# Both attention stages of a hybrid layer: low halves moved to GpSimd, and second operands of VectorE moved to PSUM

## What is computed

```python
def block(args):                      # group A, stick-breaking
    i, qi = args
    q_pos = i * Q_BLOCK + jnp.arange(Q_BLOCK)
    z = jnp.einsum('bhqd,bhkd->bhqk', qi, k).astype(jnp.float32) * inv_sqrt_d
    strict = key_pos[None, :] < q_pos[:, None]
    log_keep = jnp.where(strict, jax.nn.log_sigmoid(-z), 0.0)
    after = lax.cumsum(log_keep, axis=3, reverse=True) - log_keep
    w = jnp.where(strict, jnp.exp(jax.nn.log_sigmoid(z) + after), 0.0)
    return jnp.einsum('bhqk,bhkd->bhqd', w.astype(v.dtype), v)
...
    p = jax.nn.softmax(jnp.where(causal, z, neg), axis=-1)      # group B
    return jnp.einsum('bhqk,bhkd->bhqd', p.astype(v.dtype), v)
...
mixed = jnp.concatenate([o_sb, o_mla], axis=-1)
return x + gate * (mixed @ w_out)
```

## Time and profile before

| | us |
|---|---|
| median of the runs | 2296.2 |
| the profiled execution | 2294.13 |
| its span, first to last instruction | 2292.2 |
| TensorE busy | 1953.2 (85%) |
| VectorE busy | 1397.9 (61%) |
| ScalarE busy | 942.5 (41%) |
| GpSimd busy | 604.3 (26%) |

### The profile page before, as it was taken

One profiled execution on the slowest core, in us unless ns is written; L12 is line 12 of the kernel. 1 busy time (PEld: TensorE's weight loads), 2 busy tenths in 40 slices (PEclk: granted clock), 3 DMA queues, 4 the chain that ended last, 5 costly groups with the idle time before them and its releaser, 6 DMA issues. The chain is left out here.

```text
span 2292.2 us, 31958 instructions
## 1 busy us (share of the span) xinstructions
PE 1953.2 (85%) x9698; PEld 1565.0 (68%) x9698; DVE 1397.9 (61%) x2006; ACT 942.5 (41%) x1836; POOL 604.3 (26%) x515
## 2 busy tenths in 40 slices
PE   6489999969995777389898988969999999995998
PEld 1368888859994666367676766748777787774786
DVE  2811111121112788499999999969899898984111
ACT  1411111122222344256666666636566576663000
POOL 1400000000000455300000000027677777772222
PEclk9699999989997999689999999969999999997999
DMA  7235553344443466652532414091243440404664
GB/s 284 92 122 162 171 155 106 119 173 157 171 169 128 135 197 202 195 124 49 129 74 73 112 33 115 14 197 40 53 111 83 105 88 19 111 10 156 188 187 156
DMA packets 220768, 284.58 MB, mean 124 GB/s; under 512 B 11216, under 2 KB 158976, under 8 KB 215024
## 3 DMA queue, kind: packets, MB, share of 16 engines
q1 hardware_dynamic: 215344, 270.77, 40.7%
q10 hardware_dynamic: 5312, 12.58, 1.6%
HBM read 164.56 MB, written 114.56 MB: 122 GB/s over the span
## 5 line engine op out<-in xcount | busy, mean ns | idle before, releaser
L1895 POOL TENSOR_TENSOR mla_wl<-mla_w,mla_wh 128x512 fp32r<-128x512 f32 (+1 forms) x280 | 382.3, 1382 | 165.4 <-ACT mla_wh L1932 163.1
L1995 DVE TENSOR_TENSOR mla_acc<-mla_acc,mla_w 128x512 f32<-128x512 f32 (+3 forms) x288 | 271.6, 943 | 38.6 <-ACT mla_w L1930 35.7
L1513 DVE TENSOR_TENSOR_SCAN sb_w<-sb_kp,sb_w 128x512 f32<-128x512 f32 x192 | 245.2, 1277 | 7.3 <-ACT sb_kp L1463 0.9
L1472 ACT ACTIVATE sb_wh<-sb_pt 128x512 fp32r<-128x512 f32 (+1 forms) x320 | 170.5, 533 | 149.5 <-PE sb_pt L1605 145.7
L1930 ACT ACTIVATE mla_w<-mla_zt 128x512 f32<-128x512 f32 (+1 forms) x320 | 170.6, 533 | 140.3 <-PE mla_zt L2082 68.1
L515 PE MATMUL pt_po<-h_hi,pt_wh 128*128 128x512 f32 x512 | 200.1, 391 | 9.3 <-DVE pt_wl L476 9.3
L517 PE MATMUL pt_po<-h_hi,pt_wl 128*128 128x512 f32 x512 | 199.9, 390 | 0.0
L516 PE MATMUL pt_po<-h_lo,pt_wh 128*128 128x512 f32 x512 | 199.9, 390 | 0.0
L1973 DVE TENSOR_REDUCE mla_nmx<-mla_zn 128x1 f32<-128x512 f32 (+2 forms) x320 | 191.4, 600 | 11.0 <-PE mla_zn L2048 7.9
L1463 ACT ACTIVATE sb_kp<-sb_z 128x512 f32<-128x512 f32 (+3 forms) x320 | 169.7, 531 | 53.4 <-PE sb_z L1583 23.2
L1583 PE MATMUL sb_z<-sb_kk,sb_qh 128*128 128x512 f32 (+3 forms) x320 | 146.3, 457 | 33.5 <-DMA sb_ql<-qk_sb 27.1
(11 more groups left out here) (220 smaller groups left out, 4130.0 us busy)
## 6 DMA issues: line engine op xcount, KB each, us to landing
pn_hs<-hT SPq DMA_DIRECT2D x16, 1024.0 KB, 4.8
mod_wada<-in_w_ada SPq DMA_DIRECT2D x6, 2048.0 KB, 8.3
qk_mla<-lat_th SPq DMA_DIRECT2D x32, 384.0 KB, 4.3
qk_mla<-lat_tl SPq DMA_DIRECT2D x32, 384.0 KB, 5.1
mod_x<-in_x ACTq DMA_DIRECT2D x16, 512.0 KB, 4.1
pt_w<-in_w_feat SPq DMA_DIRECT2D x16, 512.0 KB, 6.0
hT<-h_hi SPq DMA_DIRECT2D x16, 512.0 KB, 3.5
hT<-h_lo SPq DMA_DIRECT2D x16, 512.0 KB, 5.2
```

Of the source, the lines that this page charges most:

```text
L1472: nc.scalar.activation(wh[x % RING][:, lo:GW], pt[x % PTS][:, lo:GW], ACT.Copy, bias=-1.0).then_inc(s_hi if plan.split[x] else s_whole, 1)
L1513: nc.vector.tensor_tensor_scan(kept, keeps, keeps, 1.0 if u["n"] == 0 else w[u["g"]][:, u["r"], b:b + 1], ALU.mult, ALU.bypass).then_inc(s ...
L1895: nc.gpsimd.tensor_tensor(wl[i][:, cols], w[i][:, cols], wh[i][:, cols].bitcast(F32), ALU.subtract).then_inc(s_lo, 1)
L1995: nc.vector.tensor_tensor(a[:, cols], a[:, cols], w[x % RING][:, cols], ALU.add).then_inc(s_acc, 1)
```

## The change

In SB the scan's second, ignored operand becomes `beside`, a PSUM bank that VectorE fills with zeros once. The PSUM bank comes from `pt`, which has three now instead of four. All turns are split. In three turns of four ScalarE writes a float32 `wf`, GpSimd rounds it into `wh` and subtracts into `wl`; in the fourth ScalarE rounds and VectorE subtracts, as it did before in the other three. The product comes three turns after the transposes instead of two. The epilogue's `finish` comes one turn later, `mh` is made by ScalarE one turn after that (`high`), and `ml` by VectorE another turn later (`low`).

In MLA the running sum is kept in a PSUM bank `pa` until the diagonal turns, of which the first reads `pa` and writes `acc` in SBUF. That bank is the former `pm`; the transposed maxima now use `ps`, with new waits: `to_row` for `scale` of the group before, `over_keys` for the row. Every turn is split.

```diff
-    WHOLE = (3,)
...
+    def pooled(self, x):
+
+        return x % self.RING != self.RING - 1
...
-    PTS = 4
+    PTS = 3
...
-        wh = [m.sb(f"wh{i}", [P, GW], F32 if i in plan.WHOLE else F32R) for i in range(RING)]
-        wl = [None if i in plan.WHOLE else m.sb(f"wl{i}", [P, GW], F32R) for i in range(RING)]
+        wf = [m.sb(f"wf{i}", [P, GW]) for i in range(RING - 1)]
+        wh = [m.sb(f"wh{i}", [P, GW], F32R) for i in range(RING)]
+        wl = [m.sb(f"wl{i}", [P, GW], F32R) for i in range(RING)]
...
+        beside = m.ps("beside", [P, GW])
...
-        AFTER = 3
-        ends = {plan.groups[n]["turns"] - 1 + AFTER: n for n in range(G - 1)}
+        AFTER = 4
...
+            def turn(it, x):
+                if not plan.pooled(x):
+                    return
+                lo, i = plan.turns[x]["lowest"] * P, x % RING
+                pooled = it * plan.pooled_to(T - 1) + plan.pooled_to(x)
+                pool.wait_ge(s_whole, pooled)
+
+                reached(pool, s_pv, it * T + x + 1 - RING)
+                pool.sem_inc(s_step, 1)
+                nc.gpsimd.tensor_copy(wh[i][:, lo:GW], wf[i][:, lo:GW]).then_inc(s_phi, 1)
+                pool.wait_ge(s_phi, pooled)
+                nc.gpsimd.tensor_tensor(wl[i][:, lo:GW], wf[i][:, lo:GW], wh[i][:, lo:GW].bitcast(F32),
+                                        ALU.subtract).then_inc(s_plo, 1)
...
-                reached(act, s_pv, k + 1 - RING)
-                nc.scalar.activation(wh[x % RING][:, lo:GW], pt[x % PTS][:, lo:GW], ACT.Copy,
-                                     bias=-1.0).then_inc(s_hi if plan.split[x] else s_whole, 1)
+                if plan.pooled(x):
+
+                    reached(act, s_plo, it * plan.pooled_to(T - 1) + plan.pooled_to(x - RING))
+                    nc.scalar.activation(wf[x % RING][:, lo:GW], pt[x % PTS][:, lo:GW], ACT.Copy,
+                                         bias=-1.0).then_inc(s_whole, 1)
...
-                nc.vector.tensor_tensor_scan(kept, keeps, keeps,
+
+                nc.vector.tensor_tensor_scan(kept, keeps, beside[:, 0:b - a],
...
-                if not plan.split[x]:
+                if plan.pooled(x):
                     return
...
-                nc.vector.tensor_copy(mh[b][:], om[:, cols]).then_inc(s_mh, 1)
...
-                if not plan.split[x]:
-                    nc.tensor.matmul(out, vj.bitcast(F32), wh[x % RING][:, lo:GW], start=tn["first"],
-                                     stop=tn["last"]).then_inc(s_pv, 1)
-                    return
...
-            LAG = 2
+            LAG = 3
...
-    WHOLE = 8
-
...
-        pm = m.ps("pm", [P, GW])
+        pa = m.ps("pa", [P, GW])
...
+                into = a if tn["diag"] else pa
+                came = a if tn["lowest"] else pa
+                nc.vector.tensor_tensor(into[:, cols], came[:, cols], w[x % RING][:, cols], ALU.add).then_inc(s_acc, 1)
...
                 reached(pe, s_row, groups(n, it, hp))
+
+                reached(pe, s_scale, groups(n, it, hp) - (1 if n == 1 else 2))
                 for r in range(QG):
-                    tp = nc.tensor.transpose(pm[0:1, r * P:(r + 1) * P], nm[n % 2][:, r:r + 1], ident[:])
+                    tp = nc.tensor.transpose(ps[0:1, r * P:(r + 1) * P], nm[n % 2][:, r:r + 1], ident[:])
...
                 reached(pe, s_scale, groups(n, it, hp))
+
+                rows = groups(n, it, hp) + (2 if n == G - 1 else 3)
+                reached(pe, s_row, min(rows, 2 * PAIRS * G) if isinstance(rows, int) else rows)
```

More of the change, by code:

```diff
@@ L1291, in __init__, with pooled_to, others_to, due @@
         self.rest = [(x, 1) for s in self.slots for x, back in s if back]
-    def splits_to(self, x):
-        return sum(self.split[:x + 1])
+    def pooled(self, x):
+        return x % self.RING != self.RING - 1
+    def pooled_to(self, x):
+        return x + 1 - (x + 1) // self.RING
+    def others_to(self, x):
+        return (x + 1) // self.RING
+    def due(self, x, after):
+        ends = [(n, grp["turns"] - 1 + after) for n, grp in enumerate(self.groups)]
+        return [(n, when // self.T) for n, when in ends if when % self.T == x]
     def turns_through(self, group):
@@ L1449, in _, with body @@
                                     channel_multiplier=-1).then_inc(s_const, 1)
+            def turn(it, x):
[10 more added lines that the diff above has]
+                                        ALU.subtract).then_inc(s_plo, 1)
+            def body(it, start):
+                for x in range(T):
+                    turn(it, x)
+            pairs(pool, body)
         @block.scalar
@@ L1484, in slot @@
                     turn(it - back, x)
[L1485 to L1488, removed]
+                    group_ends(it - back, x)
             def body(it, start):
@@ L1496, in _ @@
             slot(PAIRS, plan.rest)
-            half_sum(PAIRS - 1, G - 1)
+            for x in range(AFTER + 2):
+                group_ends(PAIRS, x)
         @block.vector
         def _(dve):
+            nc.vector.memset(beside[:], 0.0).then_inc(s_beside, 1)
+            dve.wait_ge(s_beside, 1)
             def unit(it, n):
@@ L1549, in slot @@
                     turn(it - back, x)
-                    if x in ends:
-                        finish(it - back, ends[x])
-                    elif x == AFTER - 1 and not (isinstance(it, int) and it - back == 0):
-                        finish(it - back - 1, G - 1)
+                    group_ends(it - back, x)
             def body(it, start):
@@ L1561, in _ @@
             slot(PAIRS, plan.rest)
-            finish(PAIRS - 1, G - 1)
+            for x in range(AFTER + 2):
+                group_ends(PAIRS, x)
         @block.tensor
@@ L1676, in __init__ @@
         self.T, self.G = len(self.turns), len(self.groups)
-        self.splits = sum(tn["split"] for tn in self.turns)
-    def splits_to(self, x):
-        return sum(tn["split"] for tn in self.turns[:x + 1])
     def at(self, x, kinds, delays):
@@ L2093, in product @@
                 out, vj = po[tn["n"] % 2][:, lo:GW], v[hp][:, tn["j"], :]
-                if not tn["split"]:
-                    pe.wait_ge(s_w, turns(x, it, hp) + 1)
-                    nc.tensor.matmul(out, vj.bitcast(F32), w[x % RING][:, lo:GW], start=tn["first"],
-                                     stop=tn["last"]).then_inc(s_pv, 1)
-                    return
-                pe.wait_ge(s_lo, split_turns(x, it, hp))
+                pe.wait_ge(s_lo, turns(x, it, hp) + 1)
                 nc.tensor.matmul(out, vj, wh[x % RING][:, lo:GW], start=tn["first"], stop=False)
```

89 lines of the change are left out of this document (58 added, 31 removed).

## The result

The changed kernel takes **2244.5 us** (median of 4 runs, 2241.1 to 2248.7), against 2299.5 for the kernel before on the same chip (4 runs, 2294.6 to 2303.4): a ratio of 0.976, with an interval of 0.973 to 0.979. It is faster by 55 us where 75 were forecast; 2244.5 lies in the range of 2170 to 2285, 25 us above the forecast of 2219. The profiled execution has a span of 2247.0 us (before 2292.2), and the spans are compared from here on.

The account below looks back on a forecast made before the run. VectorE was taken to bound SB, and TensorE MLA, with VectorE at 90% making it stumble. From 2294.1 us, SB's 40 and MLA's 35 (10 + 30 - 5) off gave 2219 us, range 2170 to 2285.

Parts of the forecast that it names:

- 2: Rival, SB: GpSimd's cast costs as much as its subtraction, so the kernel is slower, 2300 to 2340 us; chance 0.12.
- rival 3: SB: cast at the memset's price or quicker scans, so SB runs at TensorE's pace of 410 us; 2169 us; chance 0.08.
- 1: Rival, SB: GpSimd and VectorE hold each other up, only MLA gains; 2250 to 2290 us; chance 0.20.
- Scans unchanged: SB, VectorE: the scans keep their price, 348 us in all, with the ignored operand moved to PSUM.
- VectorE in SB: VectorE loses most low halves and the cast to `mh`, saving 102 us, and needs 403 us.
- GpSimd in SB: Its 240 turns need 279 us of subtractions, 151 of casts and 12 of hand-overs, 442 us.
- for moments when GpSimd finds no turn ready I add 10: SB: 10 us for GpSimd starved, as three engines lie within 10%; SB then ends at 1461 us.
- So SB becomes GpSimd's: SB: GpSimd's 442 us exceed VectorE's 403 and set the stage's end, 40 us earlier.
- MLA, the products: TensorE drops 24 full fp32 products at 0.40 us each, 10 us on the path.
- The new waits on `ps`: MLA: maxima share bank `ps` with the sums, so TensorE waits for ScalarE; at most 19 us, taken as 5.
- The adds: MLA, VectorE: 192 full-width adds cost 0.42 us less each with the sum in PSUM, 81 us less.
- MLA, the recovered stops: TensorE wins back two thirds of its 32 us of waits and 15 us of clock loss: 30 us.

Follow-up runs that it names:

- runs 1 and 2: The change's SB stage with the MLA of the kernel before: 2272.5 us; the change's MLA with the SB of the kernel before: 2272.7 us.
- run 3: The change with the scan's ignored second operand read from SBUF again, against the change: 2437.1 us, 193 more.
- run 9: Run 5's kernel with SB's `mh` and `ml` also one turn later: 2201.6 us, 10 less than run 5.
- runs 10 to 12: ScalarE makes `wh` of all pooled turns, on the change: 2259.9 us; of one in three, on run 9: 2228.2; same, reading `wf` in SBUF: 2235.5.
- run 8: The change with every eighth MLA product again one fp32 matmul, halves still made: 2250.1 us, 5.6 more than the change.
- run 7: SB as in the change, MLA as before (sum in SBUF) but all turns split: 2284.5 us, against 2272.5 with the unsplit turns.
- run 5: The change with MLA's `mh` and `ml` one turn later: 2211.2 us, 33 less than the change.
- run 6: The kernel before with only MLA's `mh` and `ml` one turn later: 2289.1 us, 13 less than the kernel before beside it.

## Why the prediction was right, and where its sizes were off

**The direction and the shape held.** SB lost most of TensorE's wait for `wl` and ends earlier; MLA lost VectorE's slow adds; the gains add up (runs 1 and 2). Of the rivals, 2 fell by the cast's 640 ns (0.68 forecast, 1.1 the point from which it decides), 3 by that cast, dearer than the memset, and the unchanged scans, 1 by the subtraction's 1311 ns.

**Scans unchanged:** right to a nanosecond or two. But I priced the PSUM operand by what it gives the scan, nothing, and missed what it prevents: run 3 shows that it is worth 193 us beside GpSimd's new work. The row that the forecast needed, a scan beside GpSimd, was not in the trace of before, where GpSimd is idle in SB. My 1.28 us for the subtraction rested on the sentence that almost no VectorE operation would have two SBUF operands; with the operand left where it was, that sentence would have been false.

**VectorE in SB:** forecast 403 us, measured 421. The 128-column low half is 274 ns (0.27). The epilogue's steps became dearer beside GpSimd (972 against 693 ns for L1599, 910 against 692 for L1611, 8 us in all), and less of the rest overlaps.

**GpSimd in SB:** forecast 442 us. It works from 1001.3 to 1467.8 us with 25 us of waits for ScalarE, so 441. That the sum fits to 1 us is luck: subtractions took 287 for 279, casts 143 for 151, and the instructions overlap enough that starts follow each other every 1.93 us (median) where 2.01 was forecast for a full turn. What failed is the step "for moments when GpSimd finds no turn ready I add 10": it is 25, and that, with 4 us for the last epilogue (6 forecast), makes 1472 of 1461. Level engines starve each other more than their surplus says. Part of it is ScalarE's new wait before `high`, which I had called a step with room on ScalarE's side: run 9 takes it a turn later, and SB's last `ml` starts at 1459. TensorE was mis-sized as well: forecast near 410 us, busy 446, the busiest of the three, so the pace of 410 that rival 3 wanted was not there. "So SB becomes GpSimd's" fell with runs 10 to 12: it is level, and ScalarE's order bears on its pace as GpSimd's work does.

**MLA, the products:** 10 us forecast, 5.6 to 8.3 in run 8, hardly clear of its noise. **The new waits on `ps`:** 5 us forecast; no row of weight appears for TensorE's `ps` (2.7 us for the reciprocals, 7.2 before). **The adds:** 75 us less on VectorE (192 x 0.39) for the 81 forecast, and 40 us of the kernel (run 7).

**MLA, the recovered stops:** this is the step that failed: "these stops come where VectorE is late, so I take two thirds, 30". The three waits fell by 9.6 us of 32, and the clock, from which I hoped to win, went from 0.97 to 0.95. I had listed ScalarE's 37.3 us before `mh` in the earlier trace rows and given it no term, since TensorE was the bound and ScalarE two thirds busy. But ScalarE executes in order: 16 stops of 1.6 us each (2.3 before) hold back the exponentials, TensorE runs dry a turn later, and behind the gaps it runs at the lower clock for a while (at 1603 us, above). Run 5 moves `mh`, with `ml` behind it, by one turn and gives 33 us, more than the 4 (by the medians of run 2) to 16 us (by the two traces) that MLA misses; its MLA, 540.6 us against 595.3, is near the "57 less" that the prediction gave for all waits and the clock. Run 6 shows that most of this could not be had before the adds were fast.

## What to carry to other kernels

A step of an epilogue that waits on an in-order engine costs what stands behind it, not its own time: give it its input a turn early, and read its wait with its count even where its engine has room. Before work moves to GpSimd, look at VectorE's operations beside it: here the move paid with at most one of the scan's operands in SBUF and cost 193 us more with two, and an operand that is ignored counts. Where three engines come within a few per cent of each other, allow more for starvation than for the surplus of the slowest, and test a relief by what it puts into the queue of the engine that takes over.

## What the runs showed of the hardware that was not expected

An ignored second operand (`ALU.bypass`) of VectorE's scan in SBUF slows GpSimd and the scan as a used one does: the scan went from 1278 to 1674 ns, GpSimd's one-operand cast from 640 to 1233, its subtraction from 1311 to 1649 (run 3 against the change). The cast suffers more than the subtraction, by 593 ns against 338.

TensorE's granted clock fell from 1.00 to 0.50 behind the second of two gaps, 1.34 and 1.06 us (0.85 from 1596 to 1606 us of the change), and with these gaps gone it stayed at 1.00 over 460 us (run 5).
